# Mixer's first product: ScalarE and VectorE take one pair, the next weight chunk, and then the other pairs behind the norm's factor

## What is computed

```python
x = x + 0.5 * rms_norm(swiglu(h, ffn1_w_gate, ffn1_w_up, ffn1_w_down), ffn1_post_g)
h = rms_norm(x, mix_pre_g)
proj = h @ w_in
q, k, v, z, xbc, dt = jnp.split(proj, IN_SPLITS, axis=-1)
...
xbc = jax.nn.silu(causal_depthwise_conv(xbc, conv_w, conv_b))
...
h = rms_norm(x, ffn2_pre_g)
x = x + 0.5 * rms_norm(swiglu(h, ffn2_w_gate, ffn2_w_up, ffn2_w_down), ffn2_post_g)
```

## Time and profile before

| | us |
|---|---|
| median of 3 runs (1383.39 to 1383.76) | 1383.43 |
| the profiled execution | 1381.03 |
| its span | 1379.2 |
| TensorE busy in the span | 1317.9 (96%) |
| VectorE busy | 793.6 (58%) |
| ScalarE busy | 617.5 (45%) |
| GpSimd busy | 173.1 (13%) |

### The profile page before, as it was taken

How to read it: one execution, slowest core, us unless ns; L and a number is a source line. 1 busy time by engine, 2 the same in 40 slices (tenths; PEclk the granted TensorE clock), 3 DMA queues, 4 the chain that set the end, 5 groups by cost and what they waited for, 6 DMA issues and landing times.

```text
span 1379.2 us, 23104 instructions
## 1 busy us (share of the span) xinstructions
PE 1317.9 (96%) x9908; PEld 1226.2 (89%) x9908; DVE 793.6 (58%) x1062; ACT 617.5 (45%) x936; POOL 173.1 (13%) x224
## 2 busy tenths in 40 slices
PE   5999999999999999999999999998799888999997
PEld 5997669999999868999999999998797558999996
DVE  5745446555456465556454766547755765766643
ACT  5424445554333354554345444444544534544432
POOL 4000002110000001111011111010402401011101
PEclk8999999999999999999999999999999959999999
DMA  6571004555636502455544454563252006255461
GB/s 253 215 248 61 1 31 148 183 183 191 206 132 205 187 7 92 156 183 205 194 160 167 163 184 163 189 207 142 94 201 69 1 1 221 94 187 182 146 208 71
DMA packets 33494, 204.45 MB, mean 148 GB/s; under 512 B 3552, under 2 KB 5872, under 8 KB 13168
## 3 DMA queue, kind: packets, MB, share of 16 engines
q1 hardware_dynamic: 33392, 202.97, 42.8%
HBM read 201.89 MB, written 1.07 MB: 147 GB/s over the span
## 4 chain that ended last, share of the span: by engine, by line
PE 83%; DVE 7%; issue 6%; ACT 3%; POOL 1%; DMA 0%; SPq 0%; POOLq 0%; ACTq 0%; DVEq 0%
PE ps L614 22%; PE ps L615 22%; PE ps L616 22%; PE ps L884 3%; DVE wl L567 2%; PE ps L635 1%; PE ps L636 1%; PE ps L637 1%; PE ps L885 1%; PE ps L836 1%; PE ps L1280 1%; PE ps L1278 1%; POOL acc L699 1%; PE ps L2189 1%; ACT wh L559 1%
## 5 line engine op out<-in xcount | busy, mean ns | idle before, releaser
L567 DVE TENSOR_TENSOR wl<-raw,wh 128x2048 fp32r<-128x2048 f32 (+3 forms) x201 | 429.1, 2139 | 212.5 <-ACT wh L559 212.2
L614 PE MATMUL ps<-xh,wh 128*128 128x256 f32 x1712 | 492.1, 287 | 34.4 <-DVE xl L689 17.2
L615 PE MATMUL ps<-xl,wh 128*128 128x256 f32 x1712 | 489.8, 286 | 0.0
L616 PE MATMUL ps<-xh,wl 128*128 128x256 f32 x1712 | 489.5, 286 | 0.0
L559 ACT ACTIVATE wh<-raw 128x2048 fp32r<-128x2048 f32 (+3 forms) x201 | 357.3, 1782 | 208.6 <-PE ps L616 179.2
L614 PEld LDWEIGHTS ps<-xh,wh 128*128 128x128 f32 x1712 | 334.5, 195 | 37.3 <-issue 25.1
L615 PEld LDWEIGHTS ps<-xl,wh 128*128 128x128 f32 x1712 | 334.4, 195 | 0.0
L616 PEld LDWEIGHTS ps<-xh,wl 128*128 128x128 f32 x1712 | 334.2, 195 | 0.0
L614 PE MATMUL ps<-ah,wh 128*128 128x256 f32 x1088 | 309.6, 285 | 1.1 <-DVE wl L567 1.1
L615 PE MATMUL ps<-al,wh 128*128 128x256 f32 x1088 | 308.8, 284 | 0.0
L616 PE MATMUL ps<-ah,wl 128*128 128x256 f32 x1088 | 308.7, 284 | 0.0
(11 more groups left out here) (323 smaller groups left out, 1314.5 us busy)
## 6 DMA issues: line engine op xcount, KB each, us to landing
raw<-wstream SPq DMA_DIRECT2D x157, 1024.0 KB, 4.9
raw<-wstream SPq DMA_DIRECT2D x32, 704.0 KB, 4.1
raw<-wstream SPq DMA_DIRECT2D x8, 768.0 KB, 4.2
e_bt<-scratch SPq DMA_DIRECT2D x4, 512.0 KB, 6.6
raw<-wstream SPq DMA_DIRECT2D x2, 560.0 KB, 5.5
consts<-consts SPq DMA_DIRECT2D x1, 1025.0 KB, 9.9
raw<-wstream SPq DMA_DIRECT2D x4, 256.0 KB, 5.2
h<-xt SPq DMA_DIRECT2D x4, 256.0 KB, 5.8
```

What stands on the lines that cost most here:

```text
L567: e.g.tensor_tensor(WL[q][:, 0:w], RAW[i % RAWN][:, 0:w], f32(WH[q][:, 0:w]), ALU.subtract).then_inc(S["lo"], 1)
L614: e.g.matmul(o, wh[:, sl], xh[:, cs], start=start, stop=False, skip_group_check=pair)
L615: e.g.matmul(o, wh[:, sl], xl[:, cs], start=False, stop=False, skip_group_check=pair)
L616: ins = e.g.matmul(o, wl[:, sl], xh[:, cs], start=False, stop=k == p.nk - 1, skip_group_check=pair)
```

## The change

In `count`, a product with `G.fixed` gets its list in another order: behind `after` comes the first pair, then the first event of `late` (the next chunk), then the other early pairs, then the rest. And VectorE goes through `mu` with `behind` 0 instead of 1.

```diff
--- before.py
+++ after.py
@@ -347,7 +347,11 @@
         at = G.events.index(early[-1])
         late = G.events[at + 1:]
         G.events = [x for x in G.events[:at] if x not in early]
-        G.events += [("after", max(i for kind, i in G.events if kind == "chunk"))] + early + late
+        G.events += [("after", max(i for kind, i in G.events if kind == "chunk"))]
+        if G.fixed:
+            G.events += [early[0], late.pop(0)] + early[1:] + late
+        else:
+            G.events += early + late
         chunk += G.chunks
     ends.sort()
     return [e for _, e in ends]
@@ -1964,7 +1968,7 @@
                 if pair == 0:
                     taps_u(5)
 
-            dve_gemm(e, G["mu"], 1, after=dve_finish(5, 1e-6, then=scaled(32.0 ** -0.5)), drain=drain_u)
+            dve_gemm(e, G["mu"], 0, after=dve_finish(5, 1e-6, then=scaled(32.0 ** -0.5)), drain=drain_u)
             dve_gemm(e, G["mz"], 1, drain=drain_z)
             dve_gemm(e, G["mn"], 0, drain=dve_narrow(G["mn"], 5))
             dve_gemm(e, G["mq"], 0, drain=dve_to(G["mq"], m_q, 5, by=5))
```

## The result

The change makes the kernel slower: 1390.43 us (median of 4 runs, 1389.16 to 1391.68) against 1383.41 us for the kernel before in the same comparison, ratio 1.0055 (95% interval 1.0043 to 1.0068). Forecast was 1390.1 us, slower.

A forecast was written before the change was run, and what follows sets the result against it. TensorE, busy 96% of the span, was taken as the bound, with a 7.43 us wait ahead of chunk 145. Terms 5.6 (mixer) + 0 (clock) + 1.1 (gate product) = +6.7 us gave 1390.1 us, range 1386.5 to 1394.5.

The forecast's parts named there:

- Chunk 145 on time, 146 the new wait: Mixer's first product: chunk 145 starts 7.59 us earlier, but an 8.7 us wait ahead of 146 replaces the 7.43 one.
- the sum: Step-by-step timeline of mu from pair 0's drain at 961.04 to chunk 148's start at 1001.81, 5.6 us late.
- taps(5): VectorE's convolution taps of pair 5 in mu, directly ahead of chunk 148's low half, forecast from 996.76 to 999.38.
- VectorE stands for the high half: In mu VectorE idles about 3.3 us before chunks 146 and 147, their high halves lying behind the SiLUs on ScalarE.
- The clock behind the last wait: TensorE's clock after the 3.4 us wait ahead of chunk 148: cost 0 or up to 2.3 us, taken as 0.
- rival 1: Clock drops behind the 3.4 us wait ahead of chunk 148: +9.0 us in all, 1392.4 us; chance 0.34.
- the 4.98 us wait: Earlier TensorE wait in the kernel before, followed by 5.2 us at clock 0.50, costing 2.3 us.
- The gate product: Second gate product: chunk 170's earlier high half on ScalarE delays its low half; wait 1.8 instead of 0.69 us, +1.1 us.
- Together: Whole kernel: 5.6 for mu, 0 for the clock, 1.1 for the gate product, +6.7 us, 1390.1 us.
- The faster rival: In mu the first wait goes and nothing comes back, hand-overs lying beside VectorE's work: −7.8 us, 1375.6 us; chance 0.07.
- The 8.9 us: Gain open at chunk 145 in mu: the 7.43 us wait plus 1.50 us of slow clock behind it.

The follow-up runs named there:

- run 10: Changed kernel with VectorE's two taps of each mu tile over 8 of 256 columns, the rest left out; 1381.2 us, 0.9995 of the kernel before.
- run 5: Changed kernel, but ScalarE makes the high halves of chunks 146 and 147 one pair earlier, ahead of pairs 3 and 4; 1382.3 us, ratio 1.0006 to before.
- run 1: Kernel before with only the second edit, VectorE going through mu with `behind` 0 in the old order of events; 1389.5 us, ratio 1.0057.
- run 3: Whole change in mu alone, gate2 in its old order, against the kernel before; 1388.1 us, ratio 1.0053.
- run 12: Kernel before with VectorE's mu low halves interleaved between pairs, each high half behind the same pair's first taps on ScalarE; 1380.1 us, ratio 0.9989.
- run 4: Kernel before with the new order of events in gate2 alone, mu as before; 1383.5 us, ratio 1.0011.
- run 6: Kernel before with separate mu lists: VectorE's low halves ahead of pairs' taps, ScalarE's high halves a pair earlier; 1370.3 us, ratio 0.9922.
- run 8: Kernel before with only ScalarE's interleaved mu list of run 6, VectorE's list and `behind` 1 kept; 1385.9 us, ratio 1.0022.
- run 9: Kernel before with VectorE's two taps of each mu tile over 8 of 256 columns, the rest left out; 1379.5 us, ratio 0.9980.

## Why the prediction was right, point by point

- **Chunk 145 on time, 146 the new wait.** Right. Forecast 8.7, 1 and 3.4 us ahead of 146 to 148, measured 8.53, 0.72 and 3.12. Against the first drain (961.04 before, 963.82 after) chunk 148 started at 1001.53, where the sum had 1001.81: 5.3 us late instead of 5.6. Of the 0.3, 0.2 are taps(5), 2.50 us instead of 2.70.
- **VectorE stands for the high half.** Right and shown: 3.27 us each (forecast 3.4 and, for the second, the same), 3.26 and 3.27 with short taps (run 10), gone with the high half a pair earlier (run 5), back with it behind (run 12).
- **The clock behind the last wait.** The term of the sum that was wrong. I took 0 for it, with up to 2.3 as the bound and rival 1 for that end. The profile shows 0.50 (the 1.2 GHz level) for 2.5 us behind the wait of 3.12 us. Chunk 148 took 7.15 us (1004.31 to 1011.46) instead of 5.76, so it cost 1.4. The profiles of runs 1 and 3 show the same behind waits of 3.10 us. Behind 2.58 us and, in run 1, behind 2.11 us the clock stayed at 1.00. So rival 1 was right on the fact, and its 2.3 us, taken from the 4.98 us wait, was too large for this one. The Trainium skill's rule of no gap above about 3 us (TensorE: Matmul & The Clock Gate, "Why this matters for your kernels") agrees with these waits. It does not cover run 12, where the clock fell with no gap above 2.12 us.
- **The gate product.** Forecast +1.1, measured 1.84 − 0.69 = 1.15 us in the wait (the working gave 1.2 us for lo(170), entered as 1.1), and runs 3 and 4 put it where it was forecast. With hi(170) gone from its old place the last low half's wait was 0.79 us again, as supposed.
- **Together.** 5.3 + 1.4 + 1.15 = 7.8 us in the profile against 6.7 forecast and 7.0 in the medians. That the medians lie nearer to the forecast than the profile is luck: single runs of one kernel scatter by more than the clock term, and with this term in the sum the forecast would have been 8.1. The order of events, the stands and the gate product were foreseen; the clock was not.

Of the 10.7 us between the two profiled executions 2.9 lie ahead of the product (first matmul 937.79 and 940.64) and have nothing to do with the change. In the profiles of all fourteen kernels here this matmul starts between 937.55 and 940.78; run 4, whose only edit acts far behind it, has it at 940.15. About half of the 2.9 us arises in the stretch from 31 to 70 us, here in the kernel before, and then after (window, us, TensorE busy, granted clock, ...):

```profile
31.00:70.00 39.00, 38.01 (x302) 0.96 0.54 192
```

```profile
31.00:70.00 39.00, 38.24 (x291) 0.91 0.52 190
```

The work there is the same, and the clock is lower for a longer time in the second execution. The rest arises up to 120 us; from 110 to 120 the granted clock was 0.98 and 0.85.

The faster rival had named the right goal and the wrong means. The 8.9 us that the prediction counted as open were there (S falls by 9.2 in run 6), but not by this change: it needed the two engines to have different orders, and the high halves ahead of the SiLUs.

## What to carry to other kernels

Where one engine's result feeds another's next step (a high half for a low half), give the consumer something to do between the two, or make the producer's part a step earlier; taking away the slack of one step moved the wait to the next chunk, with a stand of 3.3 us at each of the two high halves. One list of events for all engines ties together what should be apart: with a list for each engine the same work lost its wait and its slow clock (0.9922). An early step that needs a buffer which TensorE has yet to free (run 8) blocks all that lies behind it on its engine, so look at what an early instruction waits for before moving it.

## What the runs showed of the hardware that was not expected

- In run 12 the granted clock fell while TensorE worked: behind the third of three waits of 1.45, 2.12 and 2.11 us, matmuls came every 0.12 us at first and then, from about 996.6 to 1000.0, every 0.21. Each of these waits alone is shorter than the 2.58 us that left it alone.
- A longer wait did not cost more clock. A chunk that takes 5.76 us at 1.00 took 1.4 us more behind a wait of 3.12 us, 2.5 more behind 5.19 (run 9), 2.2 more behind 5.17 (run 5) and 1.5 more behind 7.43 (kernel before). What sets the length of the slow stretch is not shown.
- VectorE's instructions over 8 columns shortened little in a chain that goes over GpSimd: four of them took 1.96 us beside GpSimd's adds, against 2.70 us over 256 columns.
- Executions of one and the same kernel differ by over 5 us (run 6: 1368.14 to 1373.72) and the mean granted clock goes with it: 0.978 in the shortest and 0.970 in the longest. Why one execution has more of the low clock than another is not shown.
